# When GpSimd begins to add the squares behind attention: with the first square, or with the sixth low half of y

## The reference, cut to what matters

```python
h = jnp.concatenate([meta, x], axis=1)
for i in range(DEPTH):                        # 4 layers
    y = rmsnorm(h, norm_mix_g[i])
    ...                                       # i = 1: diff_attention(y, ...), which ends in o @ w_o
    h = h + y
    h = h + swiglu_ffn(rmsnorm(h, norm_ffn_g[i]), ffn_w_gate[i], ffn_w_up[i], ffn_w_down[i])
return rmsnorm(h[:, N_META:], final_norm_g)

def rmsnorm(x, g, eps=RMS_EPS):
    y = xf * lax.rsqrt(jnp.mean(xf * xf, axis=-1, keepdims=True) + eps)
    return (y * g.astype(jnp.float32)).astype(x.dtype)

def swiglu_ffn(h, w_gate, w_up, w_down):
    return (jax.nn.silu(h @ w_gate) * (h @ w_up)) @ w_down
```

## Time and profile before

| | |
|---|---|
| median of 3 runs | 2052.43 us (2052.23 to 2052.7) |
| the profiled execution | 2053.15 us |
| its span, first to last instruction | 2051.4 us |
| mean granted TensorE clock | 0.992 of full speed |
| busy: TensorE, VectorE, ScalarE, GpSimd | 98%, 77%, 43%, 11% |
| of the chain that ended last: TensorE, VectorE, ScalarE | 87%, 6%, 2% |

### The profile page before, as it was taken

One profiled execution on the slowest core, in us unless ns is written; L12 is line 12 of the kernel. 1 busy time (PEld: TensorE's weight loads), 2 busy tenths in 40 slices (PEclk: granted clock), 3 DMA queues, 4 the chain that ended last, 5 costly groups with the idle time before them and its releaser, 6 DMA issues.

```text
span 2051.4 us, 40665 instructions
## 1 busy us (share of the span) xinstructions
PE 2013.0 (98%) x16006; PEld 1944.3 (95%) x16006; DVE 1575.3 (77%) x2277; ACT 883.9 (43%) x1376; POOL 226.5 (11%) x332
## 2 busy tenths in 40 slices
PE   7999999999999999999999999999999999999998
PEld 7999999988888899999999999999999988999997
DVE  6797778766776779777977896687787757977794
ACT  6443334334444534333438764343343334433342
POOL 5000000412122200000051111100000160000000
PEclk9999999999999999999999999999999999999999
DMA  5423333332111223333336641233342422233332
GB/s 165 136 83 103 100 105 95 91 105 63 50 48 51 78 83 95 99 94 102 98 108 134 135 109 52 79 87 94 112 122 63 125 72 83 83 103 102 102 104 93
DMA packets 304266, 195.14 MB, mean 95 GB/s; under 512 B 7098, under 2 KB 296891, under 8 KB 303892
## 3 DMA queue, kind: packets, MB, share of 16 engines
q1 hardware_dynamic: 298972, 175.08, 29.8%
q0 software_dynamic: 3984, 14.08, 3.2%
q10 hardware_dynamic: 1192, 4.34, 0.5%
HBM read 179.44 MB, written 6.44 MB: 91 GB/s over the span
## 4 chain that ended last, share of the span: by engine, by line
PE 87%; DVE 6%; issue 2%; ACT 2%; POOLq 1%; DVEq 1%; DMA 0%; SPq 0%; POOL 0%; ACTq 0%
PE ps L876 42%; PE ps L1140 34%; PE ps L993 2%; PE ps L1251 2%; PE ps L934 1%; PE ps L1342 1%; PE ps L1318 1%; DVE w_lo L2024 1%; PE ps L977 1%; POOLq L770 1%; POOLq L767 1%; DVE y_lo L2030 0%; PE ps L903 0%; PE ps L1353 0%; PE ps L1329 0%
## 5 line engine op out<-in xcount | busy, mean ns | idle before, releaser
L1140 PE MATMUL ps<-t_lo,y_hi 128*128 128x264 f32 (+1 forms) x1008 | 285.7, 283 | 0.0
L1140 PE MATMUL ps<-t_lo,w_hi 128*128 128x264 f32 (+1 forms) x1008 | 285.7, 283 | 0.0
L1140 PE MATMUL ps<-t_hi,w_lo 128*128 128x264 f32 (+1 forms) x1008 | 285.5, 283 | 0.0
L1140 PE MATMUL ps<-t_hi,y_lo 128*128 128x264 f32 (+1 forms) x1008 | 285.3, 283 | 0.0
L1140 PE MATMUL ps<-t_hi,w_hi 128*128 128x264 f32 (+1 forms) x1008 | 285.1, 283 | 0.1
L1140 PE MATMUL ps<-t_hi,y_hi 128*128 128x264 f32 (+1 forms) x1008 | 284.8, 283 | 0.0
L1721 ACT ACTIVATE w_hi<-w_raw 128x1024 fp32r<-128x1024 f32 (+1 forms) x108 | 128.0, 1202 | 328.9 <-PE ps L876 192.8
L876 PE MATMUL ps<-hid_hi,w_hi 128*128 128x264 f32 (+1 forms) x1184 | 265.4, 296 | 0.5 <-DVE hid_lo L2319 0.5
L876 PE MATMUL ps<-hid_lo,w_hi 128*128 128x264 f32 (+1 forms) x1184 | 264.6, 296 | 0.0
L876 PE MATMUL ps<-hid_hi,w_lo 128*128 128x264 f32 (+1 forms) x1184 | 264.2, 296 | 0.0
L876 PE MATMUL ps<-y_hi,w_hi 128*128 128x264 f32 (+1 forms) x1088 | 243.5, 300 | 3.9 <-DVE q L2522 1.7
(11 more groups left out here) (321 smaller groups left out, 4398.4 us busy)
## 6 DMA issues: line engine op xcount, KB each, us to landing
w_raw<-in_ffn_w_gate SPq DMA_DIRECT2D x88, 512.0 KB, 5.1
w_raw<-in_ffn_w_up SPq DMA_DIRECT2D x88, 512.0 KB, 4.6
w_raw<-in_ffn_w_down SPq DMA_DIRECT2D x70, 512.0 KB, 4.3
w_raw<-in_ffn_w_down SPq DMA_DIRECT2D x24, 384.0 KB, 4.3
w_raw<-in_attn_w_qkv SPq DMA_DIRECT2D x16, 512.0 KB, 3.7
w_raw<-in_conv_w_in SPq DMA_DIRECT2D x16, 512.0 KB, 4.2
w_lo<-w_raw POOLq DMA_DIRECT2D x16, 512.0 KB, 5.1
w_raw<-in_attn_w_qkv SPq DMA_DIRECT2D x16, 256.0 KB, 2.9
```

The source lines that it names most:

```text
L1140: mm = pe.matmul(ps[:, bank, 0:hw], w[:, at:at + P], b[:, t, k, 0:hw], start=k == 0 and n == 0, stop=k == 3 and n == 2)
```

## The change

Two lines are added to `sum_squares`, the helper that GpSimd runs for each norm. They act in one of its calls. No instruction moves on any engine, and none is added but this wait.

```diff
                 elif r == R_FFN1:
                     pool.wait_ge(s.square_ready, squares_before(r) + 1)
                 pool.memset(m.sumsq[:, :], 0.0)
+                if r == R_FFN1:
+                    pool.wait_ge(s.y_ready, NB * Y_FFN1 + 6)
                 pool.drain()
                 with pool.Fori(0, NB) as d:
```

## The result

Over 20 runs each, the changed kernel takes 2063.74 us in the median (2058.64 to 2068.65) and the kernel before 2058.19 (2052.23 to 2061.47). The ratio is 1.0032, with a 95% interval of 1.0022 to 1.0041, so it is slower by 6.6 us (4.5 to 8.4). The profiled execution took 2059.09 us, with a span of 2057.4 against 2051.4: 6.0 us more.

A forecast was written before the change was run, and what follows sets the result against it. TensorE, busy 98% of the span, was taken as the bound, by its waits or lower clock. Late sums +3.75 and a half-rate spell +1.7 gave +5.45 on the 2052.43 median: 2057.9 us, 8-in-10 range 2054.7 to 2060.0.

The forecast's parts named there:

- VectorE's gain: Between attention and second feed-forward block: unheld low halves of y free TensorE's banks earlier, its idle shrinking by 1.29 us.
- First addition: GpSimd's first addition of squares, after the wait for the sixth low half of y, starts near 711.1 us.
- Holds on the additions: VectorE's remaining low half and weight splits delay GpSimd's first four additions: 0.57 us, then about 0.4 each on two.
- Late sums: TensorE's ten one-column matmuls wait 5 us for GpSimd's eighth addition, starting at 726.95 against 723.19: +3.75 us.
- The clock: After the idle and one-column sums, TensorE runs a spell at half rate: +1.7 us, bounds 0 and 3.4.
- the upper bound of 3.4: Rival: the lower clock lasts longer, as in the first 24 us, losing up to 3.4 us; 2059.6 us, chance 10%.
- The two rows: Profile rows on TensorE's clock: 1.7 us lost at the last pooling layer, at most 3.4 in the first 24 us.
- The seam's sum: Total between attention and second feed-forward block: late sums +3.75 plus lower clock +1.7 gives +5.45 us.
- The base: Whole kernel: the difference of 5.45 us was added to the median of the runs, 2052.43 us, giving 2057.9.
- the replay of VectorE and GpSimd: Between attention and second feed-forward block: instruction times recomputed, each low half at 0.76 us unless a GpSimd addition holds it.
- Chances: Whole kernel against a 0.2% line at 2056.5 us: slower 0.72, within 0.25, faster 0.03.
- slack 4.3 us: Before the change, GpSimd's eighth addition ends at 718.87, TensorE reaches the sums at 723.19: 4.3 us of room.

The follow-up runs named there:

- e2: Kernel before, with GpSimd adding only 8 of 528 columns of each square in this one norm (measurement only); ratio to the kernel before 0.9987 (0.9973 to 1.0001).
- e1: Changed kernel plus 38 full-width matmuls into a free bank ahead of the sums, where TensorE else idles; ratio to the kernel before 1.0017 (1.0000 to 1.0034).
- e4: Changed kernel with GpSimd's wait set to the fourth low half of y, not the sixth; ratio to the kernel before 1.0007 (0.9992 to 1.0022).
- e7: Changed kernel with GpSimd's wait set to the fifth low half of y, not the sixth; one run, 2059.22 us.
- e6: The changed kernel run once more, unchanged; it took 2061.19 us.

## Why the prediction was right and where it was wrong

- **VectorE's gain.** Forecast: TensorE's two waits shrink by 1.29 us in all. Measured: 2.95 us became 1.58, so they shrank by 1.37. Right; e2 gives 1.35 as the seam's whole gain.
- **First addition.** Forecast 711.1, which is 10.5 behind the memset; measured 10.35. Right.
- **Holds on the additions.** Forecast 1.4 us over the eight; measured 26.03 - 10.35 = 15.68 against 14.4 clean, 1.3. Right. The eighth ended 0.3 us earlier than forecast, counted from the memset (26.03 for 26.3).
- **Late sums.** Forecast +3.75; measured 3.46 from the memset. Right in kind and size. The wait was 4.63 us for a forecast of 5.
- **The clock.** Forecast +1.7, taken from the last pooling layer. Measured +3.04. The mechanism was right, as e1 shows, but this term was mis-sized: the row was one behind an idle of 1.29 us and the case had 4.63. The kernels e4 and e7, with idles of 1.55 and 3.38, lost 1.6, as the pooling layer did; the changed kernel lost about twice that, near the upper bound of 3.4 from the earlier trace rows, for which I had given 10%. That the longer idle is what made the spell longer is not shown: 3.38 us cost no more than 1.55, and at 38 to 50 us one and the same wait was followed by a loss of 3.4 us in e6 and 5.1 in e1. The two rows gave 1.7 and 3.4, and nothing in them said which would come.
- **The seam's sum.** Forecast 3.75 + 1.7 = 5.45; measured 3.46 + 3.04 = 6.50. The late sums were 0.29 too high and the clock 1.34 too low. That the medians differ by 5.55, so near the forecast, is luck: they are medians of runs that spread over 10 us, and their ratio gives 6.6.
- **The base.** This is the step that put the time out of the range: "so I add to the median". Three runs within 0.5 us looked like a kernel that repeats to 0.02%, and I took them for the level. They were at the lowest level of those that its runs fall into. Over 20 runs the median of the kernel before is 2058.19 and not 2052.43. That is 5.76 us of the 5.8 between the forecast of 2057.9 and the 2063.7 measured, and the stated range had no term for it. The trace of before held a warning: TensorE has a 3.0 us wait at 656, longer than the 1.29 behind which the clock fell at 1664, and the clock did not fall there. In seven of the ten other traces it did.
- **The Trainium skill's rule on the clock** (TensorE: Matmul & The Clock Gate, section "Why this matters for your kernels"), that a gap in TensorE's work brings half rate, was the part that spoke against the change; this case bears it out, 3.04 of 6.50 us. The Trainium skill's lock of the shared ports (SBUF — State Buffer, section "SBUF: two separate sides"), where the one that starts first keeps the ports and the other waits, carried the replay of VectorE and GpSimd. The trace agrees: the starts of the additions and low halves that the prediction gives came out within 0.3 us, counted from the memset.
- **Chances.** I gave 0.72 to slower by over 0.2%; it is slower by 0.32%, the interval's lower end 0.22%.

## What to carry to other kernels

To hold a side engine back so that it doesn't disturb the critical one is worth at most the disturbance (here 1.35 us) and spends the slack at its other end; work out that end first: slack 4.3 us, delay 9.4 us, less the 1.7 us that the additions gain back by being held off less. A late result cost TensorE twice here, once as the wait and once more as a spell at half rate, and in e4 a wait of 1.55 us that hardly delayed the sums (0.38 us) cost 1.6 us that way. And before adding a difference to a base, look in the trace for waits where the clock might have fallen: the base can have levels, and here three runs were all on one.

## What the runs showed of the hardware that I had not expected

The granted clock fell in some executions and held in others at the same 3.00 us wait at 656 us of the same program, and so moved a whole run by 4 us. Where the wait was followed by the one-column sums (1.55, 3.38, 4.63 us of idle), it fell in each of the four traces, with 1.6, 1.6, 3.0 and 3.1 us of delay (e4, e7, the changed kernel and e6). With full-width matmuls in place of the idle it held at 1.00, though the one-column sums still stood there.
